# A decoder trunk in one launch: an earlier second gating, modulation pieces in pairs, and a layer norm taken half by half

## What is computed

```python
mod = einsum('bd,lde->lbe', silu(c), w_ada) + b_ada        # 9 rows, 2 layers x 6 x 1024 outputs
h = rmsnorm(x, g) * (1 + scale) + shift
a, gate = split(h @ w_in, 2)
u = a * sigmoid(gate)                                       # the gating
u = causal_depthwise_conv(u, buf, w_dw, b_dw)               # width 31, per channel
u = layernorm(u, ln_g, ln_b)                                # mean and variance over the 1024 channels
y = silu(u) @ w_out
```

## Time and profile before

| what | value |
|---|---|
| time, median of 3 runs | 1578.58 us (1577.2 to 1578.93) |
| the profiled execution | 1577.84 us, of which the span is 1576.2 us |
| TensorE busy | 1511.8 us, 96% of the span |
| VectorE busy | 1014.7 us, 64% |
| ScalarE busy | 880.5 us, 56% |
| mean granted TensorE clock | 0.989 of full speed |
| moved by DMA | 273.76 MB, mean 174 GB/s |

### The profile page before, as it was taken

One profiled execution on the slowest core, in us unless ns is written; L12 is line 12 of the kernel. 1 busy time (PEld: TensorE's weight loads), 2 busy tenths in 40 slices (PEclk: granted clock), 3 DMA queues, 4 the chain that ended last, 5 costly groups with the idle time before them and its releaser, 6 DMA issues.

```text
span 1576.2 us, 28413 instructions
## 1 busy us (share of the span) xinstructions
PE 1511.8 (96%) x11348; PEld 1368.2 (87%) x11348; DVE 1014.7 (64%) x1531; ACT 880.5 (56%) x1627; POOL 138.6 (9%) x364
## 2 busy tenths in 40 slices
PE   5999999999999999999999998999999999999997
PEld 4777754989999999999979975668999999999997
DVE  4889993679664488754625544665578654677743
ACT  4454565678663486644524645664587653566632
POOL 1000000000000033200000012110000000232200
PEclk8999999999999999999999999999999999999998
DMA  9755575325555445554426456664145454454552
GB/s 365 283 200 210 205 265 174 122 68 174 163 185 177 137 150 168 169 193 151 161 67 221 147 174 215 214 215 166 54 134 173 163 192 156 138 171 167 190 174 97
DMA packets 71764, 273.76 MB, mean 174 GB/s; under 512 B 8032, under 2 KB 10096, under 8 KB 71120
## 3 DMA queue, kind: packets, MB, share of 16 engines
q1 hardware_dynamic: 65248, 246.44, 45.7%
q0 software_dynamic: 6096, 25.15, 4.8%
q10 hardware_dynamic: 288, 0.35, 0.1%
HBM read 262.80 MB, written 8.85 MB: 172 GB/s over the span
## 4 chain that ended last, share of the span: by engine, by line
PE 78%; DVE 13%; ACT 5%; issue 3%; DMA 2%; DVEq 0%; ACTq 0%
PE ps L674 59%; PE ps L904 3%; DVE odd_taps L1739 3%; DVE y L1739 3%; PE ps L651 2%; DVE w_lo L1562 2%; PE ps L742 2%; PE ps L940 1%; PE ps L957 1%; PE ps L963 1%; PE ps L720 1%; PE ps L1024 1%; DVE y L1839 1%; PE ps L991 1%; ACT w_hi L1153 1%
## 5 line engine op out<-in xcount | busy, mean ns | idle before, releaser
L674 PE MATMUL ps<-h_hi,w_hi 128*128 128x288 f32 x1920 | 572.1, 298 | 11.2 <-DVE w_lo L1562 8.5
L674 PE MATMUL ps<-h_hi,w_lo 128*128 128x288 f32 x1920 | 566.4, 295 | 0.0
L674 PE MATMUL ps<-h_lo,w_hi 128*128 128x288 f32 x1920 | 566.4, 295 | 0.0
L1562 DVE TENSOR_TENSOR w_lo<-raw,w_hi 128x1024 fp32r<-128x1024 f32 (+1 forms) x309 | 403.1, 1306 | 238.3 <-ACT w_hi L1153 237.7
L1153 ACT ACTIVATE w_hi<-raw 128x1024 fp32r<-128x1024 f32 (+1 forms) x309 | 347.1, 1125 | 109.3 <-PE ps L674 73.0
L674 PEld LDWEIGHTS ps<-h_hi,w_hi 128*128 128x128 f32 x1920 | 361.2, 188 | 23.0 <-DVE w_lo L1562 11.4
L674 PEld LDWEIGHTS ps<-h_lo,w_hi 128*128 128x128 f32 x1920 | 361.3, 188 | 0.7
L674 PEld LDWEIGHTS ps<-h_hi,w_lo 128*128 128x128 f32 x1920 | 361.2, 188 | 0.0
L674 PE MATMUL ps<-act_hi,w_hi 128*128 128x288 f32 x704 | 208.3, 296 | 0.0
L674 PE MATMUL ps<-act_lo,w_hi 128*128 128x288 f32 x704 | 207.7, 295 | 0.0
L674 PE MATMUL ps<-act_hi,w_lo 128*128 128x288 f32 x704 | 207.0, 294 | 0.0
(11 more groups left out here) (242 smaller groups left out, 1965.8 us busy)
## 6 DMA issues: line engine op xcount, KB each, us to landing
raw<-w_k_dram SPq DMA_DIRECT2D x245, 512.0 KB, 3.5
raw<-w_down_dram SPq DMA_DIRECT2D x64, 704.0 KB, 4.0
ada_w<-w_ada_dram SPq DMA_DIRECT2D x72, 512.0 KB, 5.6
k_page<-cache_kt_dram SPq DMA_DIRECT2D x32, 512.0 KB, 5.3
v_page<-cache_v_dram POOLq DMA_DIRECT2D x32, 512.0 KB, 5.2
ada_h<-w_ada_dram SPq DMA_DIRECT2D x12, 512.0 KB, 7.0
ada_u<-w_ada_dram SPq DMA_DIRECT2D x6, 512.0 KB, 15.8
x<-x_in_dram SPq DMA_DIRECT2D x1, 2304.0 KB, 11.2
```

Of the source, the lines that this page charges most:

```text
L674: mm = pe.matmul(ps[:, BANK[b], 0:HALF], lhsT=w[s][:, kb * P:(kb + 1) * P], rhs=v[:, at, :] if down else v[:, at, lo:hi], start=(at == 0 a ...
L1562: dve.tensor_tensor(w_lo[s][:, 0:cols], raw[n % RING][:, 0:cols], w_hi[s][:, 0:cols].bitcast(F32), ALU.subtract).then_inc(s_lo, 1)
```

## The change

1. `EARLY_TAPS[0]` goes from 32 to 22: ten taps of chunk 0 move behind the gating of chunk 1.
2. The reused buffers become six (pieces 79 to 84) at other offsets in `h`. They leave chunks 0 and 1 of `h_hi` and of `h_lo` free. The loads wait for 3, 4, 5, 7, 7 and 7 of the seven pieces instead of 1 to 5. Eleven ring pieces follow instead of twelve.
3. Group 5 gathers in bank 7 instead of bank 6, and the transposes of groups 4 and 5 go to bank 6. The first piece of group 5 no longer waits for the copy of group 4; that copy moves behind ScalarE's loop over half 0.
4. The mean of each half lies in a bank of its own (0 and 3), is counted by itself, and is read by VectorE from there; the two copies to `mu` go. The mean of half 0 no longer waits for the decode sums.
5. VectorE's order becomes: coefficients, subtractions of half 0, decode sum of chunk 7, two subtractions of half 1, and the other two between `norm_make(2)` and the first `norm_low`.
6. In TensorE's list the mean of chunk 7, half 1, stands behind the squares of half 0. The first square sum of half 1 goes into the loop: even `kb` have one square sum, odd ones two modulation pieces. Three pieces follow the loop.
7. ScalarE and VectorE wait for the six pieces later in their loops (chunk 3 and chunk 4). The squares have two separate buffers.

```diff
-EARLY_TAPS = [WA - PE_TAPS[0] + 1] + [18] * (C - 3) + [6, 0]
+EARLY_TAPS = [22] + [18] * (C - 3) + [6, 0]
...
-OWN_AGAIN = range(OWN_TILE.stop + ADA_RING, OWN_TILE.stop + ADA_RING + 5)
+AGAIN_AT = ((4608, 3), (9216, 4), (13312, 5), (23040, 7), (27648, 7), (32768, 7))
+OWN_AGAIN = range(OWN_TILE.stop + ADA_RING, OWN_TILE.stop + ADA_RING + 6)
...
-                        sp.wait_ge(ada_done, OWN_TILE.start + j + 1)
+                        sp.wait_ge(ada_done, OWN_TILE.start + AGAIN_AT[j][1])
...
-                if n % PIECES == 0:
+                last = n // PIECES == GROUPS - 1
+                if n % PIECES == 0 and last:
+                    pe.wait_ge(mod_ready, GROUPS - 2)
+                elif n % PIECES == 0:
                     pe.wait_ge(mod_copied, n // PIECES)
...
-                pe.wait_ge(conv_seq, n + 1)
-                for h in range(2):
-                    mm = pe.matmul(ps[:, h, 0:HALF], lhsT=mean_w[:], rhs=y[:, n, h * HALF:(h + 1) * HALF],
-                                   start=(n == 0), stop=(n == C - 1))
+                if h:
+                    pe.wait_ge(conv_seq, n + 1)
+                mm = pe.matmul(ps[:, MEAN_BANK[h], 0:HALF], lhsT=mean_w[:], rhs=y[:, n, h * HALF:(h + 1) * HALF],
+                               start=(n == 0), stop=(n == C - 1))
...
             for n in range(C):
-                mean_sum(n)
+                mean_sum(n, 0)
+                if n < C - 1:
+                    mean_sum(n, 1)
             late_pieces(ADA_RING)
             for p in range(C // 2):
                 square_sum(0, p)
-            square_sum(1, 0)
+            mean_sum(C - 1, 1)
             late_pieces(len(OWN_AGAIN))
...
-                if kb in (1, 3, 5):
-                    square_sum(1, (kb + 1) // 2)
-                late_pieces(1)
+                if kb % 2 == 0:
+                    square_sum(1, kb // 2)
+                else:
+                    late_pieces(2)
...
-            act.wait_ge(a_stat, 2)
-            for h in range(2):
-                lo, hi = half_cols(h)
-                act.activation(mu[:, lo:hi], ps[:, h, 0:HALF], ACT.Copy).then_inc(a_rs, 1)
             for p in range(C // 2):
                 ln_square(0, p)
-            ln_square(1, 0)
             ln_scale(0)
+            for n in range(C + 1):
+                if n == 3:
+                    act.wait_ge(ada_done, OWN_AGAIN.stop)
+                ln_silu(n, 0)
+                if n % 2:
+                    ln_square(1, n // 2)
             copy_group(GROUPS - 2)
-            act.wait_ge(ada_done, OWN_AGAIN.stop)
-            for n in range(C + 1):
-                ln_silu(n, 0)
-                if n in (1, 3, 5):
-                    ln_square(1, (n + 1) // 2)
             ln_scale(1)
...
             early_taps(C - 1, range(0, WA - PE_TAPS[C - 1] + 1))
-            seq_conv(C - 1)
...
+            def centre(h, p):
+                lo, hi = half_cols(h)
+                dve.wait_ge(a_stat, 2 + h)
+                t = y[:, 2 * p:2 * p + 2, lo:hi]
+                dve.tensor_tensor(t, t, ps[:, MEAN_BANK[h], 0:HALF].unsqueeze(1).to_broadcast([P, 2, HALF]), ALU.subtract)\
+                    .then_inc(conv_centred, 1)
+            for p in range(C // 2):
+                centre(0, p)
+            seq_conv(C - 1)
             dve.wait_ge(conv_seq, C)
...
+            for p in range(2):
+                centre(1, p)
...
                     norm_make(1, n, 0)
+                if n == 2:
+                    for p in range(2, C // 2):
+                        centre(1, p)
                 if n >= 2:
+                    if n == 2:
+                        dve.wait_ge(ada_done, OWN_TILE.stop)
+                    if n == 4:
+                        dve.wait_ge(ada_done, OWN_AGAIN.stop)
                     norm_low(1, n - 2, 0)
```

More of the change, by code:

```diff
@@ L377, in trunk_kernel @@
                    for j in range(len(OWN_TILE))]
+        ada_again = [place(f"ada_g{j}", [P, C * P], at=[h_off + o, h_off + o + C * P * 4])
+                     for j, (o, _) in enumerate(AGAIN_AT)]
         diag_more = place("diag_more", [P, PE_TAPS[-1] - DIAG_TILE, P], at=[h_off + 7 * C * P * 4, h_off + 9 * C * P * 4])
@@ L400, in trunk_kernel @@
         c_act = place("c_act", [P, C, 32], at=at)
-        mu = place("mu", [P, TT], at=temp(shared))
+        sq_ln = [place("sq_ln0", [P, TT], at=temp(shared)), place("sq_ln1", [P, TT], at=at)]
         x_first = place("x_first", [P, TT], at=temp(shared))
@@ L454, in two @@
             return ap.rearrange("p (b t) -> p b t", b=2)
-        STAT = 2
+        STAT, MEAN_BANK = 2, (0, 3)
         def prm(name, index, count=1):
@@ L573, in ada_piece @@
                     if again:
-                        sp.wait_ge(ada_done, OWN_TILE.start + j + 1)
+                        sp.wait_ge(ada_done, OWN_TILE.start + AGAIN_AT[j][1])
                     else:
                         sp.wait_ge(gemm_done, 2 * C)
-                    sp.dma_start(ada_own[j][:], w_ada[n]).then_inc(ada_first_in[ADA_RING + j], 16)
+                    sp.dma_start((ada_again if again else ada_own)[j][:], w_ada[n]).then_inc(ada_first_in[ADA_RING + j], 16)
                     return
@@ L710, in ada_piece @@
                     pe.wait_ge(ada_first_in[ADA_RING + j], 48 if again else 32)
-                    w = ada_own[j]
+                    w = (ada_again if again else ada_own)[j]
                 else:
@@ L719, in ada_piece @@
                     t = 2 * h + j
-                    mm = pe.matmul(ps[32 * t:32 * t + 32, 6, :], lhsT=c_act[:, kb, :], rhs=w[:, j * 512:(j + 1) * 512],
+                    mm = pe.matmul(ps[32 * t:32 * t + 32, 7 if last else 6, :], lhsT=c_act[:, kb, :], rhs=w[:, j * 512:(j + 1) * 512],
                                    start=(kb == 0), stop=(kb == C - 1), skip_group_check=True)
@@ L728, in turn_group @@
                 for q in range(4):
-                    mm = pe.matmul(ps[:, 7, q * ADA_TILES * NB:(q + 1) * ADA_TILES * NB], lhsT=mod_t[:, q * P:(q + 1) * P],
+                    mm = pe.matmul(ps[:, 6 if g >= GROUPS - 2 else 7, q * ADA_TILES * NB:(q + 1) * ADA_TILES * NB],
+                                   lhsT=mod_t[:, q * P:(q + 1) * P],
                                    rhs=four_diag[:].rearrange("p a b -> p (a b)"), start=(q == 0), stop=True,
@@ L829, in square_sum @@
                 pe.wait_ge(sq_ready, h * (C // 2) + p + 1)
-                pair = two(sq[:, p % 2, :])
+                pair = two(sq_ln[p % 2][:])
                 for j in range(2):
@@ L1208, in copy_group @@
                 act.wait_ge(mod_turned, g)
-                act.activation(mod_t[:], ps[:, 6, :], ACT.Copy).then_inc(mod_copied, 1)
+                act.activation(mod_t[:], ps[:, 7 if g == GROUPS - 1 else 6, :], ACT.Copy).then_inc(mod_copied, 1)
             def first_copy(q):
@@ L1282, in ln_square @@
                     act.wait_ge(sq_used, q - 1)
-                act.activation(two(sq[:, p % 2, :]), y[:, 2 * p:2 * p + 2, lo:hi], ACT.Square).then_inc(sq_ready, 1)
+                act.activation(two(sq_ln[p % 2][:]), y[:, 2 * p:2 * p + 2, lo:hi], ACT.Square).then_inc(sq_ready, 1)
             def ln_scale(h):
@@ L1589, in bias_mod @@
                     .rearrange("p (t q b) -> p t q b", q=4, b=NB)
-                src = ps[:, 7, 0:GROUP * NB].rearrange("p (q t b) -> p t q b", q=4, b=NB)
+                src = ps[:, 6 if g >= GROUPS - 2 else 7, 0:GROUP * NB].rearrange("p (q t b) -> p t q b", q=4, b=NB)
                 dve.wait_ge(mod_turned, g + 1)
@@ L1617, in norm_make @@
                 if norm == 1:
-                    dve.wait_ge(a_rs, 4 + h)
+                    dve.wait_ge(a_rs, 2 + h)
                     dve.tensor_tensor(out, y[:, n, lo:hi], rs[:, lo:hi], ALU.mult).then_inc(hn_made, 1)
@@ L1801, in _ @@
             dve.wait_ge(taps, TAP_DONE[C - 1])
-            dve.wait_ge(conv_seq, C)
[L1803 to L1810, removed]
+            def centre(h, p):
[7 more added lines that the diff above has]
+            seq_conv(C - 1)
+            dve.wait_ge(conv_seq, C)
+            for p in range(2):
+                centre(1, p)
+            dve.wait_ge(conv_centred, C // 2)
             for n in range(C + 2):
```

4 lines of the change are left out of this document (2 added, 2 removed).

## The result

The kernel after takes 1562.77 us (median of 4 runs, 1561.14 to 1565.18), the kernel before 1577.96 beside it (4 runs, 1577.2 to 1578.93): ratio 0.9905, 95% interval 0.9887 to 0.9922. That is 15.2 us gained (12.3 to 17.8 by the interval) where 11.9 were forecast from the profiled execution of before. The profiled execution took 1561.86 us (span 1560.1, granted clock 0.994); the one of before 1577.84 (1576.2, 0.989), so the two spans differ by 16.1.

The account below looks back on a forecast made before the run. It took TensorE as three quarters of the chain that ended last, VectorE an eighth. 5.4 + 3.6 + 2.9 = 11.9 us off 1577.84 gives 1565.9; with the median 0.74 higher, 1566.7 us, range 1563 to 1571.5.

Parts of the forecast that it names:

- part 3: Loop over half 0: shortened by moving a square sum in and pairing pieces, 20.9 to 18.0 us, a gain of 2.9.
- 8 x 1.39: New loop: all eight groups of nine block matmuls counted at 1.39 us each, within its 18.0 us.
- the same 1.5: Loop's start: 1.5 us for the slow clock, kept in the new loop as in the old.
- part 1: Gating stage: without TensorE's stall at chunk 1's diagonal matmuls, all three engines stand 5.4 us earlier; low end 3.6.
- mark of failure: Signs of being wrong: half 0's mean waiting for loads or taps, waits for six pieces, `ada_w` or later weights; no size.
- rival 1: Gating stage: the diagonals' clock stays low or the stage takes back part; gain 10.1, 1568.5 us; chance 0.15.
- Part 2: Layer norm: the loop starts at 247.15 instead of 250.78 in the old trace's times, a gain of 3.6 us.
- What is late next is TensorE: Mean of half 0: TensorE, busy until 235.4, and not the taps; subtractions start at 236.15, not 238.07.
- rival 4: Loop: the clock holds into it, gaining 1.5 us more, 1565.2 us; chance 0.15.
- still waits 1.8 us: Loop's start: TensorE still waits 1.8 us there, the reason given for keeping 1.5 us of slow clock.

Follow-up runs that it names:

- e3: The kernel before with EARLY_TAPS[0] at 22 (the ten taps moved) and nothing else: 1571.17 us, ratio 0.9955.
- e8: The kernel after with both means copied to SBUF by ScalarE and subtracted from the copy: 1563.75 us, ratio 0.9914.
- e7: The kernel after with group 5 back in bank 6, transposes in bank 7, group 4's copy ahead of ScalarE's loop: 1561.89 us, ratio 0.9916.
- e2: The kernel after, unchanged, run once more: 1562.84 us, ratio 0.9902.
- e6: The kernel after with all four subtractions of half 1 ahead of the first multiplication of half 0: 1565.46 us, ratio 0.9941.
- e5: The kernel after with one piece in every pass of the loop instead of two in every odd one: 1564.17 us, ratio 0.9934.
- e1: The kernel before, unchanged, run once more: 1578.55 us, ratio 1.0001.
- e4: The kernel after with EARLY_TAPS[0] back at 32: 1570.16 us, ratio 0.9952.
- e10: e9 with two pieces also moved behind the sums over channels, so eight, not six, stand in the wait at the loop: 1561.60 us, ratio 0.9890.
- e11: The kernel after with the pairs of pieces on even places of the loop and the square sums on odd ones: 1559.76 us, ratio 0.9875.
- e9: The kernel after with ScalarE's first two high parts right behind their SiLU, VectorE's last two subtractions behind the first two low parts: 1561.26 us, ratio 0.9895.
- e12: e9 with the pairs of pieces on even places of the loop and the square sums on odd ones: 1560.58 us, ratio 0.9888.

## Why the prediction fell short, and what of it held

*The step that failed* is the adding up of part 3, the loop. It took "8 x 1.39" for the new loop, where four of the eight take 1.18 (0.8 us), and it kept "the same 1.5" for a slow clock that came in none of five profiles. Part 3 is worth about 4.7 us where it had 2.9. The second term that was too small is the 5.4 of part 1. The order of events was right, so these are errors of size.

*Right: the order of events.* Nothing of what it named as a mark of failure appeared in the kernel after: no wait for `ada_w` within the loop, none of ScalarE or VectorE for the six pieces, no new waits in later blocks. The mean of half 0 waits for TensorE and not for the taps, and the tail waits 3.45 us for piece 95.

*Part 1, 5.4 us: the size was off.* The mechanism held to the letter (diagonals 5.31 us, VectorE's wait of 0.7 to 0.8, everything shifted rigidly), and against the profiled execution the stage gained 5.5. But the term was made of one execution of a stall whose cost varies: its wait was 3.58, 3.54 and 4.31 us, the matmuls behind it took 7.12, 8.36 and 8.18. Over all the profiles it is 6.8; the timed runs of e3 say 6.8 as well, but with 4.9 to 9.3 they don't exclude 5.4. That is 1.4 of the miss, 0.8 by the clock and 0.6 by the wait, and it went the way opposite to rival 1.

*Part 2, 3.6 us: right, between two profiles that lost the clock at chunk 7.* C to D went from 41.31 to 37.64: 3.67. Within it the bounds were resolved: the PSUM operand costs nothing (e8), the bank of its own 0.65 us (e7). What is late next is TensorE, as said: VectorE waits 1.69 us for the mean (0.8 in e2 and e6, which kept the clock at chunk 7).

*Part 3, 2.9 us: short by two terms.* At full clock the new loop is 3.7 shorter than the old one. The step "8 x 1.39" for the new loop failed: four of the eight follow a square sum and take 1.18, so it is 0.8 shorter (e5). The second is "and the same 1.5 (...; I keep it ...)": the slow clock stayed in the sum of the new kernel, and rival 4, with 0.15, was what happened. Its reason was that TensorE "still waits 1.8 us"; in the five profiles with a wait of 1.67 or 1.68 us there the clock never fell. In the very trace that it read the clock was also lost behind the 2.03 us before chunk 7 and kept behind 1.79 us at 319.19, which it did not weigh. The old loop lost it in two of three profiles, so the mean worth is 1.0 and not 1.5. Part 3 measured 3.7 + 1.0 = 4.7.

*The sum.* 6.8 + 3.7 + 4.7 = 15.2, beside 15.2 and 15.1 by the medians. That they meet to 0.1 us is luck, as the intervals are 5 us wide. The misses, 1.4, 0.1 and 1.8, lay on one side, and the range, which came from rivals taken one at a time, had no room for rival 4 together with a dearer stall.

*What stays open.* How the clock fares at one landmark is a matter of the execution: the diagonals of chunk 7, in no part of the change, take 7.94 us in seven of the fourteen profiles and 6.25 in the other seven, behind the same idle time of 2.03 us. All four kernels without one or both of the parts (before, e1, e3, e4) are among the seven with 7.94, and of the ten with both only three (after, e10, e11). Whether the change alters these odds, so few profiles can't tell; the sum above takes them as equal. It is 1.7 us, of the size of what separates e9 to e12 from the kernel after. And as no profile of the old layer norm kept the clock there, it is not shown what part 2 is worth when it is kept.

## What to carry to other kernels

A stall on TensorE costs its wait and the slow clock behind it, and the second part varies from one execution to the next: take its size from several profiles before it goes into a sum, and give the range both of its ends at once. When a wait in front of a chain of matmuls is shortened, ask also whether the clock is kept behind what is left of it; in e6 the clock was worth more (1.3 us) than the added wait (1.0). Before moving an operation off a bound, look at what stands behind its consumer in that engine's queue: moving the square sum was free for TensorE and made ScalarE's splits 2.4 us later.

## What the runs showed of the hardware

**The clock against the length of the wait before it.** Fourteen profiles, by TensorE's wait and whether the matmuls behind it ran at the lower level:

| wait, us | where | clock lost |
|---|---|---|
| 0 to 0.94 | loop, e7, e9, e10, e12 | 0 of 4 |
| 1.67 to 1.68 | loop, after, e2, e4, e5, e11 | 0 of 5 |
| 1.77 to 1.79 | sums of `x_sum` (L691 in before), twice in each | 5 of 28 |
| 2.03 | diagonals of chunk 7, all | 7 of 14 |
| 2.11 | loop, before, e1, e3 | 2 of 3 |
| 2.30 | a late block, for `w_lo`, all (1085.89 in before) | 6 of 14 |
| 2.51 to 2.64 | loop, e6, e8 | 2 of 2 |
| 3.54 to 4.31 | diagonals of chunk 1, before, e1, e4 | 3 of 3 |

A loss costs 1.3 to 1.7 us at the loop and chunk 7, and 1.8 to 3.1 at chunk 1. On the whole the share of losses grows with the wait, but a wait of one length can go either way. In e1 and e3 the clock is also lost behind 1.79 and 1.78 us, 41 us behind the turn, where the granted clock of the stretch is 0.83 and in before 1.00, and the way to the end is 1.5 longer. Nor does it take one long wait: in the kernel after the granted clock is 0.57 from 909 to 917 us, and from 896 us to there TensorE has no wait above 0.6. The row of that stretch in e1, and then in before:

```profile
318.00:328.00 10.00, 8.21 (x49) 7.91 (x49) 7.45 (x16) 6.85 (x16) 0.00 (x0) 0.83 0.00 1
```

```profile
318.00:328.00 10.00, 8.81 (x64) 8.70 (x65) 7.94 (x17) 6.77 (x14) 0.00 (x0) 1.00 0.01 2
```

**Two pieces for the price of one.** Eight matmuls of a pair (32 columns of weights each) take 0.99 us and four of one piece 0.98, and the next 128-column matmuls pay 0.21 once for either.

**A PSUM operand costs VectorE nothing here**: 2.75 us for four subtractions of 128x576 with it (after), 2.77 with both operands in SBUF (e8).
